# A 32-expert layer on one core: experts as a stream of pairs, the next pair's gather inside the current pair

## What is computed

```python
def hier_moe(h, w_group, b_group, w_router, b_router, w_gate, w_up, w_down):
    ...
    gates = jnp.sum(jax.nn.one_hot(e_idx, N_EXPERTS) * wts[..., None], axis=1)
    out = jnp.zeros_like(ht)
    for e in range(N_EXPERTS):
        hid = jax.nn.silu(ht @ w_gate[e]) * (ht @ w_up[e])
        out = out + gates[:, e:e + 1] * (hid @ w_down[e])
    return out.reshape(b, s, d)
```

## Time and profile before

| | |
|---|---|
| median of 3 runs | 1653.04 us (1651.25 to 1657.5) |
| profiled execution, span | 1649.2 us; what lies around the span isn't listed apart. The median is 3.8 us above the span |
| first gather starts | 600.95 us |
| last scatter starts | 1626.88 us |
| busy PE / DVE / ACT | 1440.4 / 567.9 / 167.3 us |
| mean TensorE clock that was granted | 0.963 of full |

### The profile page before, as it was taken

One profiled execution on the slowest core, in us unless ns is written; L12 is line 12 of the kernel. 1 busy time (PEld: TensorE's weight loads), 2 busy tenths in 40 slices (PEclk: granted clock), 3 DMA queues, 4 the chain that ended last, 5 costly groups with the idle time before them and its releaser, 6 DMA issues.

```text
span 1649.2 us, 15819 instructions
## 1 busy us (share of the span) xinstructions
PE 1440.4 (87%) x6490; PEld 800.4 (49%) x6490; DVE 567.9 (34%) x924; ACT 167.3 (10%) x449; POOL 23.1 (1%) x29
## 2 busy tenths in 40 slices
PE   4579999987799869889889889989989988988985
PEld 3138888776588753344335325325325335335331
DVE  2015554527644442142151242232233233133134
ACT  2000000026400110000001001001000000001001
POOL 1000000000100010000000000000000000000000
PEclk9689999999999979999999999999999999999998
DMA  9999999991488607997997997997997998999992
GB/s 347 393 393 389 385 368 361 382 374 66 142 269 309 237 26 327 425 428 292 425 427 304 426 426 306 428 426 301 430 424 316 426 426 362 404 428 389 374 424 92
DMA packets 108460, 572.33 MB, mean 347 GB/s; under 512 B 5768, under 2 KB 61208, under 8 KB 62472
## 3 DMA queue, kind: packets, MB, share of 16 engines
q1 hardware_dynamic: 106360, 567.10, 85.7%
q0 software_dynamic: 2064, 4.73, 1.0%
HBM read 569.63 MB, written 2.18 MB: 347 GB/s over the span
## 4 chain that ended last, share of the span: by engine, by line
PE 59%; DMA 23%; issue 11%; DVE 4%; ACT 2%; SPq 1%; POOL 0%; DVEq 0%; ACTq 0%; POOLq 0%
PE PS L1159 20%; DMA ring<-in_w_up 12%; PE PS L1180 11%; PE PS L1129 8%; PE PS L1145 7%; PE PS L1016 6%; DMA ring<-in_w_ada 5%; DMA ring<-in_w_qkv 5%; PE PS L1025 2%; DVE W L887 1%; PE PS L1060 1%; DMA r<-in_x 1%; PE PS L967 1%; DVE W L688 1%; PE PS L1067 1%
## 5 line engine op out<-in xcount | busy, mean ns | idle before, releaser
L1159 PE MATMUL PS<-ring,r 128*64 128x512 f32 x2048 | 449.6, 595 | 43.4 <-DMA ring<-in_w_up 32.2
L1159 PEld LDWEIGHTS PS<-ring,r 128*64 128x64 f32 x2048 | 159.1, 137 | 322.1 <-issue 322.1
L1180 PE MATMUL PS<-ring,W 128*64 128x512 f32 x1024 | 235.3, 613 | 26.8 <-DVE W L887 17.6
L1016 PE MATMUL PS<-r,ring 128*128 128x256 f32 x800 | 175.4, 382 | 3.8 <-DMA ring<-in_w_qkv 3.8
L1016 PEld LDWEIGHTS PS<-r,ring 128*128 128x128 f32 x800 | 152.7, 191 | 27.0 <-DMA ring<-in_w_qkv 4.4
L688 DVE SCALAR_TENSOR_TENSOR W<-ring,sm,W 128x2048 f32<-128x2048 f32 x60 | 141.1, 2351 | 66.8 <-DMA ring<-in_w_ada 65.3
L1180 PEld LDWEIGHTS PS<-ring,W 128*64 128x64 f32 x1024 | 76.3, 140 | 164.6 <-issue 139.4
L863 DVE TENSOR_TENSOR r<-r,PS 128x512 f32<-128x512 f32 x128 | 88.0, 687 | 183.6 <-PE PS L1129 183.6
L1129 PE MATMUL PS<-W 128*128 128x512 f32 x256 | 130.1, 648 | 21.3 <-DVE W L887 21.3
L887 DVE TENSOR_TENSOR W<-PS,W 64x1024 f32<-64x1024 f32 x64 | 78.2, 1222 | 151.9 <-PE PS L1180 151.0
L1145 PE MATMUL PS<-W,r 128*128 128x256 f32 x512 | 117.2, 391 | 3.6 <-DVE W L855 3.6
(11 more groups left out here) (184 smaller groups left out, 653.2 us busy)
## 6 DMA issues: line engine op xcount, KB each, us to landing
ring<-in_w_gate SPq DMA_DIRECT2D x64, 2048.0 KB, 21.4
ring<-in_w_up SPq DMA_DIRECT2D x64, 2048.0 KB, 25.3
ring<-in_w_down SPq DMA_DIRECT2D x64, 2048.0 KB, 22.8
ring<-in_w_ada SPq DMA_DIRECT2D x48, 2048.0 KB, 24.8
ring<-in_w_qkv SPq DMA_DIRECT2D x17, 2048.0 KB, 21.0
ring<-in_w_o SPq DMA_DIRECT2D x8, 2048.0 KB, 8.3
ring<-u_scr SPq DMA_DIRECT2D x2, 2048.0 KB, 18.0
r<-in_x SPq DMA_DIRECT2D x1, 2048.0 KB, 12.9
```

Of the source, the lines that this page charges most:

```text
L1016: last = mm(ps[:, sub * T:(sub + 1) * T], w[:, t, sub * P:(sub + 1) * P], hT[:, t, :], start=(t == 0), stop=(t == KT - 1))
L1159: last = mm(PS[64 * j:64 * j + 64, i % 2, :].rearrange("p (m n) -> p m n", m=2), hT[:, k, i * SLOTS:(i + 1) * SLOTS], w[:, :, t, 256 * j:2 ...
L1180: last = mm(PS[64 * q:64 * q + 64, 4 + i2, :], hidT[:, b, 64 * j:64 * j + 64], w[:, b, 512 * ch:512 * ch + 512], start=(j + b == 0), stop= ...
```

## The change

The mixture is reordered, and its selection works on pairs of experts.

- `GROUP` with its passes of four becomes `STREAM`, one list over all 32 experts: gate_up(0), gate_up(1), down(0), gate_up(2), down(1), and so on; down(i-1) always follows gate_up(i). SP takes the chunks in this order. The hardware loops of PE, DVE and ACT are written out.
- `BATCHES` are 16 pairs. `build_sel(b)` makes a selection of 2x64 = 128 columns for each half; `gather(b)` runs once for each pair, with a moving operand of 128 columns, in four groups of four tiles t. So there are 16 gathers of 32 matmuls where there were 8 gathers of 32.
- `gather(b+1)` stands after down of the current pair's first expert, straight before gate_up of the next pair's first. Its result goes to `hTb`, two buffers in the place of `hT`.
- All 16 tiles of a gather are evicted by ACT (`hg_evac`, 128 columns each); DVE evicts none.
- The scatter of pair b-1 comes after gate_up of pair b's second expert, and the `over` test of the routing stands behind the first build_sel on DVE.

```diff
+STREAM = ([(0, k) for k in range(4)]
+          + [c for i in range(1, E) for c in [(i, k) for k in range(4)] + [(i - 1, 4), (i - 1, 5)]]
+          + [(E - 1, 4), (E - 1, 5)])
...
-            def hg_evac(g):
-                for i in range(0, KT // 2, 2):
-                    act.wait_ge(ga_ps, 8 * g + i + 1)
-                    for t in (2 * i, 2 * i + 1):
-                        last = A.activation(hT[:, t, :], PS[:, 2, t % 2 * T:(t % 2 + 1) * T], ACT.Identity,
+            def hg_evac(b):
+                for i in range(4):
+                    act.wait_ge(ga_ps, 4 * b + i + 1)
+                    for t in range(4 * i, 4 * i + 4):
+                        last = A.activation(hTb[b % 2][:, t, :], PS[:, 2 + i % 2, t % 4 * P:(t % 4 + 1) * P], ACT.Identity,
                                             scale=A2[:, t:t + 1], bias=B2[:, t:t + 1])
...
+            for i in range(E):
+                b = BATCH[i]
+                if BATCHES[b].index(i) == 1:
+                    if b:
+                        acc_add(b - 1)
+                    if b + 1 < NB:
+                        build_sel(b + 1)
+                silu_up(i)
+                if i:
+                    result(i - 1)
+            result(E - 1)
+            acc_add(NB - 1)
...
+            def gather(b):
 
-                pe.wait_ge(sel_ok, 4 * g + 4)
-                for i in range(KT // 2):
+                pe.wait_ge(sel_ok, 4 * b + 4)
+                if b:
+                    pe.wait_ge(selT_ok, b)
+                for i in range(4):
                     if i >= 2:
-                        pe.wait_ge((hg_act, hg_dve)[i % 2], 4 * g + i // 2)
-                    for r in range(2):
+                        pe.wait_ge(hg_ok, 4 * b + i - 1)
+                    for t in range(4 * i, 4 * i + 4):
                         for h in range(H):
-                            last = mm(PS[:, 2 + i % 2, r * T:(r + 1) * T], x1[:, h, 2 * i + r::KT], selr[:, h],
+                            last = mm(PS[:, 2 + i % 2, t % 4 * P:(t % 4 + 1) * P], x1[:, h, t::KT], selr[:, h],
                                       start=(h == 0), stop=(h == H - 1))
                     last.then_inc(ga_ps, 1)
...
+            def gate_up(i):
...
+                pe.wait_ge(hg_ok, 4 * b + 4)
+                if i >= 2:
+                    pe.wait_ge(hid_ok, i - 1)
...
+            gather(0)
+            for i in range(E):
+                b = BATCH[i]
+                at_ = BATCHES[b].index(i)
+                gate_up(i)
+                if at_ == 1:
+                    if b:
+                        scatter(b - 1)
+                    sel_transpose(b)
+                if i:
+                    hid_transpose(i - 1)
+                    down(i - 1)
+                if at_ == len(BATCHES[b]) // 2 and b + 1 < NB:
+                    gather(b + 1)
+            hid_transpose(E - 1)
+            down(E - 1)
+            scatter(NB - 1)
```

More of the change, by code:

```diff
@@ L572, in hg_evac, with selT_evac @@
                                             scale=A2[:, t:t + 1], bias=B2[:, t:t + 1])
-                    last.then_inc(hg_act, 1)
-            def selT_evac(p):
-                act.wait_ge(st_ps, p + 1)
+                    last.then_inc(hg_ok, 1)
+            def selT_evac(b):
+                act.wait_ge(st_ps, b + 1)
                 A.activation(selT, PS[:, 2, 0:T], ACT.Copy).then_inc(selT_ok, 1)
[L579 to L601, removed]
@@ L1146, in _ @@
                                       start=(h == 0), stop=(h == H - 1))
                     last.then_inc(ga_ps, 1)
[L1148 to L1156, removed]
-                            k = half * (KT // 2) + t
-                            for j in range(2):
-                                last = mm(PS[64 * j:64 * j + 64, i % 2, :].rearrange("p (m n) -> p m n", m=2),
-                                          hT[:, k, i * SLOTS:(i + 1) * SLOTS], w[:, :, t, 256 * j:256 * j + 256],
-                                          start=(k == 0), stop=(k == KT - 1))
-                        last.then_inc(pe_chunk, 2)
@@ new lines, in hid_transpose, with down @@
+            def hid_transpose(i):
+                pe.wait_ge(hid_ok, i + 1)
+                for c in range(2):
+                    last = nc.tensor.transpose(PS[:, 3, c * P:(c + 1) * P], hid[:, c * P:(c + 1) * P], ident)
+                last.then_inc(hd_ps, 1)
+            def down(i):
+                pe.wait_ge(hidT_ok, i + 1)
+                if i:
+                    pe.wait_ge(yd_ok, YD[i])
+                for j in range(2):
+                    w = slot(chunk_at(AT[i, 4 + j])).rearrange("p (b n) -> p b n", b=2)
+                    for r in range(2):
+                        for i2 in range(2):
+                            for q in range(2):
+                                ch = 2 * i2 + q
+                                last = mm(PS[64 * q:64 * q + 64, 4 + i2, :], hidT[:, r * P + 64 * j:r * P + 64 * j + 64],
+                                          w[:, r, 512 * ch:512 * ch + 512], start=(j + r == 0), stop=(j + r == 2))
+                    last.then_inc(pe_chunk, 1)
```

178 lines of the change are left out of this document (89 added, 89 removed).

## The result

The changed kernel takes 1719.78 us (median of 4 runs, 1717.61 to 1720.99), the kernel before 1654.88 us beside it: a ratio of 1.0404, 95% interval 1.0382 to 1.0426. The forecast was 1704 us, slower, within 1672 to 1732. The profiled execution took 1719.16 us, its span is 1716.8 us.

The account below looks back on a forecast made before the run. Neither engine nor transfers alone bound the kernel before; PE would after. First gather at 599.95, first pair to 668.1, fourteen pairs of 67.26, end 1694.1, plus 6.3 clock: span 1700.4, plus 3.8 gives 1704 us; range 1672 to 1732.

Parts of the forecast that it names:

- The gather: 64 records at 128 columns, once per pair: 14.21 us, taken from L967, with a range of 7.15 to 14.34.
- the sign: Whole kernel: slower than before, chance 0.88; faster by over 0.5% 0.09, same 0.03.
- The rule of the Trainium skill on lines of 16 bytes: Gather's weight load: each access to a new SBUF line costs extra, so the gather costs what L967 costs.
- an estimated 6.8 us for the gather: Skill's load rule, columns divided by 1.2 in ns, backing the rival that gather time follows columns: 1591 us, chance 0.07.
- The pair: One period of two experts in the stream on PE's timeline: 51.17 plus 16.09 for gather and wait, 67.26 us.
- The waits for `yd` and for the ring: PE's waits in the mixture for DVE's result and for transfers: all go, 71.1 us in the second sum.
- the transfers kept up: Ring transfers: 12 chunks take 58.9 us, less than a pair's 67.26; the tightest chunk is there about 10 us early.
- The wait behind the gather: gate_up waiting for four ACT evictions of 128 columns: 1.48 us plus 0.40, so 1.88 us.
- The clock: Slow stretches behind the 15 waits after gathers: 6.3 us in all, bounds 0 and 25.
- One slow stretch in four: Behind waits of 1.88 us after gathers: one in four followed by a slow stretch of 1.69 us.
- the clock falls after every gather: Rival: each of 15 waits behind a gather costs 1.69 us of clock, 19 us more, 1723 us; chance 0.13.
- The sum: Whole profiled execution: all steps and the clock make a span of 1700.4 us, 51 above 1649.2.

Follow-up runs that it names:

- contig: Changed kernel plus a rewrite of the token buffer by ACT and GpSimd so the gather's weights lie side by side; 1587.31 us, ratio 0.9606.
- hide: Changed kernel with the next pair's gather ahead of the first expert's down, selection transposes and build_sel moved behind that pair's first gate_up; 1665.37 us, ratio 1.0086.
- fine: Changed kernel with the gather in eight groups of two tiles instead of four of four, two evictions behind the last group; 1682.87 us, ratio 1.0189.
- contig_wait: Changed kernel with side-by-side gather weights, plus ACT evicting the last group of four tiles twice, the first time into scratch; 1641.87 us.
- quad2: Changed kernel's stream with one 256-column gather per four experts ahead of a down, no token rewrite, first build_sel behind the overflow test; 1575.79 us, ratio 0.9542.

## Why the prediction was right, and where it was off

**The gather.** This was the step that decided the sign. It was priced from the row with the same stationary operand (L967, 14.21 us) and not from the one with the same count of columns only (L1021, 7.15 us). It measured 14.24 us. contig, which takes only the stride away, measured 7.49 us, so the mechanism is shown. L1021 was described wrongly: its stationary operand is `hT[:, t, h * P:(h + 1) * P]`, 128 tokens side by side, and the weights of the ring are the moving one; its elements lie side by side all the same, so the reading stands. The rule of the Trainium skill on lines of 16 bytes stands on the page "SBUF — State Buffer" in the section "Door 1: The DMA port swizzle (why `[64,N]` ≈ `[32,N]`)", not in the one that the prediction names. The two numbers agree with it in direction; it gives no size. The rule of the Trainium skill in "TensorE: Matmul & The Clock Gate", section "LDWEIGHTS (loading the stationary operand)", an estimated 6.8 us for the gather, is near contig's 7.49 and leaves out what a stride costs.

**The pair.** 736.08 - 669.02, a pair whose gate_up ran at the full clock, is 67.06 us; the forecast was 67.26, with 0.28 too much in its wait. The waits for `yd` and for the ring went as argued, and the transfers kept up.

**The wait behind the gather** was put at 1.88 us and is 1.60: the four evictions take 1.51 us (ACT in the second window above), as sized, but the wait is only 0.1 us longer than they are, not 0.40. Over 16 gathers that is 4.5 us too much.

**The clock is the term that was mis-sized.** One slow stretch in four was allowed, 6.3 us; 13 of 15 came, 23.3 us, with 1.7 behind the first gather: 25.0 us. The price of one was about right, 1.69 against a mean of 1.8; how often was not. I read it off the length of the wait alone, between 1.39 us (none) and 2.2 us (five of eight). The rival "the clock falls after every gather", at 1723 us, is in substance what happened. The trace of the kernel before already spoke against the length alone: PE waited 2.7 us for the ring eight times, and one of these waits had a slow stretch behind it.

```profile
1078.91 7.09 PE L1159 MATMUL PS<-ring,r 128*64 128x512 f32 x32 [2.70 <-DMA ring<-in_w_up]
...
1209.12 8.78 PE L1159 MATMUL PS<-ring,r 128*64 128x512 f32 x32 [2.70 <-DMA ring<-in_w_up]
```

The runs put five cases side by side, slow stretches of the 15 inside the stream, each counted in one profiled execution, with the mean time from gather to gather:

| gather | wait behind it | slow | gather to gather |
|---|---|---|---|
| 14.2 us, waits for its weight loads | none (hide) | 0 | 65.1 us |
| the same | 0.90 us (fine) | 2 | 66.6 us |
| the same | 1.60 us (the change) | 13 | 68.6 us |
| 7.5 us, dense (contig) | 1.60 us | 0 | 60.3 us |
| the same | 2.99 us (contig_wait) | 15 | 63.7 us |

So the standstill is needed, and the same standstill costs clock behind one gather and none behind the other. That what PE did ahead of it is the reason is the likely reading, not a shown one. Dense and 7.5 us long go together here, and so does the time from gather to gather; none of the three was held fixed. Nor do wait and foregoing work settle the single case: before the last down PE waits 2.25 us behind like rows in the change (first row) and in fine (second row), and only the first is slow.

```profile
1685.24 8.69 PE L1193 MATMUL PS<-ring,W 128*64 128x512 f32 x32 [2.25 <-issue]
```
```profile
1649.94 7.09 PE L1193 MATMUL PS<-ring,W 128*64 128x512 f32 x32 [2.25 <-issue]
```

The counts are no thresholds, then. The waits of 1.39 us before lay behind gathers that were dense in columns, and said little about sparse ones.

**The sum.** 1700.4 - 4.5 (waits) - 6.3 + 25.0 (clock) + 1.6 (the last down, slow as well: 8.69 us) = 1716.2, against 1716.8 measured. The median lies 3.0 us over the span, not 3.8. That 1719.78 falls just inside the 1690 to 1720 of the forecast is partly luck: 20.3 us of clock were missing, and 4.5 us too much of wait took some of that back. The sign was not luck, since it hangs on the gather.

## What to carry to other kernels

Price a narrower matmul by its weight load as well as by its columns, and read the load off a row with the same operand and the same step: under 256 columns of float32 a strided stationary operand cost 0.36 us of 14.3, under 128 it doubled the time. Splitting a batch in two for a smoother pipeline doubles the number of its weight loads; the smoothing was worth 4 to 5% here, and came free once the gathers were kept few (quad2) or cheap (contig). When PE has to stop behind sparse work, put another stage between the last matmul and its reader: here 25.6 us of waits came with another 25.0 us of clock.

## What the hardware did that was not expected

That 0.70 us of wait decided over some 20 us of clock inside the stream is the first thing (fine against the change). The second is in contig. GpSimd's second copy, of half the tokens, made a DVE operation on 8 columns 3.72 us long on the routing's path; the same line takes 0.17 us for 16 columns later on, and the same operation takes 0.17 us in the change. DVE and GpSimd in contig's timeline:

```profile
586.92 3.60 POOL L453 COPY r<-r 128x4096 f32<-128x4096 f32 x1 [1.25 <-DMA m_scr<-W]
587.26 0.16 DVE L805 TENSOR_REDUCE W<-W 128x2 f32<-128x8 f32 x1
587.46 3.08 DVE L806 TENSOR_TENSOR W<-W 128x8 f32<-128x8 f32 x1
...
590.97 3.72 DVE L809 TENSOR_TENSOR W<-W 128x8 f32<-128x8 f32 x1
591.04 3.62 POOL L456 COPY r<-r 128x2048 f32<-128x2048 f32 x1
...
596.57 0.17 DVE L809 TENSOR_TENSOR W<-W 128x16 f32<-128x16 f32 x1
```

Both times the DVE operation ends when GpSimd's copy does. The Trainium skill ("Advanced Engine Details and Errata", section "GPSIMD Details") says that GpSimd shares a read and a write interface with DVE and conflicts with its instructions that have two SBUF inputs; the trace agrees: both held operations have two such inputs, and the reduction at 587.26, with one, takes 0.16 us in the middle of the first copy. The second copy costs some 3.5 us, which is about the 3.4 us by which contig's first gather starts late. The first copy with its 3.08 us is in every kernel here, before the change too. And a strided copy on GpSimd took 3.62 us for 2048 columns where a plain one took 3.60 for 4096: the step doubled the cost of a column, much as it doubled that of the gather.
